# Two transformer blocks on one core: the input loaded a second time with features on rows, and down products that open their own banks

## Chip, cores and metric

One Trainium2 chip, one of its cores. The metric is the device time of one execution in microseconds (us), given as the median of several runs; the execution under the profiler is one run more and has a time of its own.

## What is computed

The input x is 256 tokens by 1024 features, float32. The first block has two layers. Each adds a mixer and then a gated feed-forward network to a residual stream, with an RMS norm ahead of both:

```python
hn = rmsnorm(x, norm_mix_w[0])
x = x + mlstm_mixer(hn, ...)                # layer 0: chunkwise mLSTM, 4 heads
x = x + swiglu(rmsnorm(x, norm_ffn_w[0]), ffn_w_in[0], ffn_w_out[0])
... # layer 1: window attention, then swiglu again

def swiglu(h, w_in, w_out):
    gu = h @ w_in                           # 1024 -> 2 * 2816
    return (silu(gu[..., :2816]) * gu[..., 2816:]) @ w_out
```

The second block joins 16 further tokens to the result, makes one wide projection of it, runs two kinds of attention and mixes them. The change touches nothing of the second block.

## The kernel before

**Exactness from two halves.** Every float32 operand of a large product is split into a rounded part (`_hi`, type float32r, written by ACT) and a rest (`_lo`, written by DVE as raw minus hi). `mm3` (lines 452 to 456) then makes each product of three matmuls: hi·hi, hi·lo, lo·hi. A weight chunk is 1024 x 512 (2 MB); it lies in `w_raw` as two halves of 1 MB, one buffer each, is split into `w_hi`/`w_lo` by ACT and DVE, and the half's buffer is free for the next transfer once DVE has written its rest (`w_lo_ok`).

**Features on partitions.** The products need activations with features on the partitions (`x_hi`, `x_lo`: 8 tiles of 128 x 256, one per 128 features, index k). The tokens lie on rows in `h`, so PE turns each tile with two transposes through PSUM (`to_stationary`, lines 512 to 526), ACT writes the hi part out of PSUM with the norm's weight as a scale (`split_st`, line 1251), and DVE writes the rest (`rest_st`, line 1747). `streamed` (528 to 543) turns two tiles ahead, and then, for each k, turns tile k+2 and does the products of tile k. The norm's root per token is not applied here: it is multiplied in later, from the sums of squares.

**The opening.** SP issues in this order (lines 351 to 361): the identity (64 KB), the parameters (40.5 KB), the two row blocks of x (512 KB each), the first half of weight chunk 0 in two pieces of 512 KB, its second half (1 MB), the side weights of the gates (512 KB). Then `main(1)` issues the two halves of chunk 1, the first once the first half of chunk 0 is split (`w_lo_ok` 1), the second once all of it is (`w_lo_ok` 2); it is followed by side unit 1 and `main(2)`. ACT (lines 1278 to 1299) waits for x and the parameters, and then for each k writes x_hi tile k, and the hi part of the weights of tile k (line 1289, 128 x 512). Behind k = 2 and k = 3 it also takes the squares of the two row blocks (line 1294). Then it splits the side unit and the two halves of chunk 1 (line 1275). DVE (lines 1812 to 1833) writes x_lo and w_lo of each k (lines 1747 and 1816); after k = 7 it raises `w_lo_ok` to 2. Then come the side unit's rest, the rest of chunk 1's first half, the roots, and the rest of chunk 1's second half (line 1808). PE does the queries' products (`halves_tile`, chunk 0: 12 matmuls of 256 columns for each k), the gates' (lines 586 to 589), and the keys' (chunk 1, lines 590 to 600), first k = 0 to 3 for both halves of the columns, then k = 4 to 7.

**The feed-forward network** (`ffn`, lines 710 to 811, called for both layers). Its down products are summed over 11 blocks of 256 features into four PSUM banks (4 to 7). The sums are opened by zero products: 16 matmuls of 128 columns from a tile of zeros, each bank's first with start set (lines 772 to 776); all products of `down` (740 to 750) then add. The zero products stand behind the last product of the mixer (`mixer_rest`, 686 to 691) and ahead of the wait for both accumulator banks (787 and 788), which the last mixer product's result leaves when DVE has added it to `h` (line 1996). Behind that wait the first up products start, with two transposes ahead of each k (`first`, 778 to 798). Then a loop of four turns does blocks 1 to 8, each `up` followed by the `down` of the block before it.

Of the kernel before, what the change touches and what calls it, by code (L numbers as in the profile page):

```python
# [20 lines left out]
F32 = mybir.dt.float32  # L21
# [5 lines left out]
P = 128  # L27
# [99 lines left out]

ST_TILES = {"x0": 8, "m_out": 8, "f0": 8, "x1": 8, "a_out": 8, "f1": 8, "u": 8, "cqkv": 3, "o_mla": 8, "o_fox": 8, "mixed": 8}

# [34 lines left out]

def two_blocks(nc, w_main, w_side, params, rows, c_l0, c_l1, c_b2, ident_d, x_d, meta_d, pos_d, out_d):
    ctx = ExitStack()
    with ctx:
# [3 lines left out]
        def sem(name):  # L171
            return ctx.enter_context(nc.semaphore(name))
# [24 lines left out]
        ffn_nat = sb("ffn_nat", [P, 2, R, 256])  # L197
        zero_r = g_hi[:, 512:512 + P]
        arena = sb("arena", [P, 17232])
# [12 lines left out]
        def pcol(name, k=0, n=1):  # L212
# [9 lines left out]

        XN = ar(4224, R, D)

        mqT, mkT, m_kn = ar(0, H0, S), ar(1024, H0, S), ar(2048, R, H0, DK)
# [55 lines left out]
        q_hi_ok, q_lo_ok, r0_ok, r0_ps, gates_ps, mk_ps, mk_ok = (  # L281
            sem(n) for n in ("q_hi_ok", "q_lo_ok", "r0_ok", "r0_ps", "gates_ps", "mk_ps", "mk_ok"))
        w_landed = [sem("w_landed0"), sem("w_landed1")]
        w_hi_ok, w_lo_ok = sem("w_hi_ok"), sem("w_lo_ok")
# [16 lines left out]
        silu_ok, g_tp, g_hi_ok, g_lo_ok = sem("silu_ok"), sem("g_tp"), sem("g_hi_ok"), sem("g_lo_ok")  # L301
        zero_ok = sem("zero_ok")
        out_landed = sem("out_landed")
# [32 lines left out]
        def _(sp):  # L336
# [13 lines left out]

            sp.dma_start(ident[:, :], ident_d).then_inc(in_landed, 16)
            sp.dma_start(par[:, :], params).then_inc(in_landed, 16)
            for r in range(R):
                sp.dma_start(h[:, r, :], x_d[r * P:(r + 1) * P, :]).then_inc(x_landed[r], 16)
            first = w_raw[:, 0, :, :].rearrange("p k n -> p (k n)")
            sp.dma_start(first[:, 0:2 * CH], w_main[0, 0][:, 0:2 * CH]).then_inc(w_first, 16)
            sp.dma_start(first[:, 2 * CH:], w_main[0, 0][:, 2 * CH:]).then_inc(w_landed[0], 16)
            main_half(0, 1)
            sp.dma_start(s_raw[:, 0, :], w_side[0]).then_inc(s_landed[0], 16)
# [36 lines left out]
        def _(pool):  # L396
            pool.memset(stat[:, :], 1.0)
            pool.memset(zero_r.bitcast(F32), 0.0).then_inc(zero_ok, 1)
            pool.memset(row_1[0:H0, :, :], 1.0)
# [51 lines left out]
        def _(pe):  # L451
# [125 lines left out]

            def m_queries(i):
                return lambda k: halves_tile(C_MQ, ("mq", i), 2 * i, k)

            pe.wait_ge(in_landed, 32)
            for r in range(R):
                pe.wait_ge(x_landed[r], 16)
            streamed("x0", residual_rows, {}, [m_queries(0), m_queries(1)])
            pe.wait_ge(s_lo_ok, U_GATES + 1)
# [4 lines left out]
            for k0 in (0, KT // 2):  # L590
                for i in range(2):
                    for k in range(k0, k0 + KT // 2):
                        ins = halves_tile(C_MK, None, 2 * i, k, to=bank[6 + i])
                    if k0:
                        ins.then_inc(mk_ps, 1)
                    elif i == 0:
                        pe.wait_ge(r0_ok, 1)
                        for r in range(R):
                            turned = pe.transpose(bank[4][:, r * P:(r + 1) * P], stat[:, 24 + r:25 + r].to_broadcast([P, P]), ident[:, :])
                        turned.then_inc(r0_ps, 1)  # L600
# [109 lines left out]
            def ffn(layer, mixer, next_st):  # L710
# [28 lines left out]

                def down(f, parts=(0, 1)):  # L740
                    pe.wait_ge(g_lo_ok, FB * layer + f + 1)
                    for ks in parts:
                        slot = (u0 + ks) % 2
                        pe.wait_ge(s_lo_ok, u0 + 2 * f + ks + 1)
                        for r in range(R):
                            for cc in range(2):
                                ins = mm3(bank[4 + 2 * r + cc][:, :], ffh[:, ks, r * P:(r + 1) * P],
                                          ffl[:, ks, r * P:(r + 1) * P], s_hi[:, slot, cc * CH:(cc + 1) * CH],
                                          s_lo[:, slot, cc * CH:(cc + 1) * CH], False, False)
                        ins.then_inc(s_used, 1)  # L750
# [19 lines left out]


                pe.wait_ge(zero_ok, 1)
                for i in range(4):
                    for q in range(4):
                        pe.matmul(bank[4 + i][:, q * P:(q + 1) * P], zero_r, zero_r,
                                  start=(q == 0), stop=False)

# [19 lines left out]
                for r in range(R):  # L797
                    for k in (KT - 2, KT - 1):
                        first(k, r)
                with pe.Fori(0, (FB - 1) // 2 - 1) as i:  # L800
                    up(2 * i + 1, 1, True)
                    down(2 * i)
                    up(2 * i + 2, 2, True)
                    down(2 * i + 1)
# [404 lines left out]
        def _(act):  # L1209
# [50 lines left out]
            def x_tile(t, a=M):  # L1260
                return lambda k: t[:, k, a:L]
# [15 lines left out]

            act.wait_ge(zero_ok, 1)
            act.activation(stat[:, 30:31], stat[:, 30:31], ACT.Square)
            for r in range(R):  # L1280
                act.wait_ge(x_landed[r], 16)
            act.wait_ge(in_landed, 32)
            for k in range(KT):
                split_st("x0", x_tile(x_hi), lambda k: pcol("norm_mix0", k), ks=(k,))
                if k == 0:
                    act.wait_ge(w_first, 16)
                elif k in (2, 4):
                    act.wait_ge(w_landed[k // 4], 16)
                act.activation(w_hi[:, 0, k, :], w_raw[:, k // 4, k % 4, :], ACT.Copy).then_inc(q_hi_ok, 1)
                if k % 4 == 3:  # L1290
                    act.drain().then_inc(w_hi_ok, 1)
                if k in (2, 3):
                    r = k - 2
                    ins = act.activation(XN[:, r, :], h[:, r, :], ACT.Square, accum_out=stat[:, r:r + 1])
                    if r:
                        ins.then_inc(ss_ok, 1)
# [420 lines left out]
        def _(dve):  # L1717
# [93 lines left out]

            dve.wait_ge(in_landed, 32)
            for k in range(KT):
                rest_st("x0", x_tile(x_hi), x_tile(x_lo), lambda k: pcol("norm_mix0", k), ks=(k,))
                dve.wait_ge(q_hi_ok, k + 1)
                dve.tensor_tensor(w_lo[:, 0, k, :], w_raw[:, k // 4, k % 4, :], w_hi[:, 0, k, :], ALU.subtract).then_inc(q_lo_ok, 1)  # L1816
                if k % 4 == 3:
                    dve.drain().then_inc(w_lo_ok, 1)
            rest_side(0)
            rest_half(1, 1, 0)  # L1820
# [844 lines left out]
```

## Time and profile before

| | us |
|---|---|
| median of 3 runs | 983.17 (982.9 to 983.58) |
| the profiled execution, its own time | 983.27 |
| its span, first to last instruction | 981.5 |
| outside the span | 1.77 |
| PE busy | 948.9 |
| DVE busy | 587.1 |
| ACT busy | 479.3 |
| POOL busy | 27.4 |

The span is what the trace covers; the profiled execution is 0.10 us above the median. A busy PE may still run at either of two clocks: the granted clock is listed as a share of 2.4 GHz for any stretch.

### The profile page before, as it was taken

What the parts mean: (1) busy time and instruction counts of PE and PEld (TensorE: products, weight loads), DVE (VectorE), ACT (ScalarE), POOL (GpSimd) and SP (SyncE); (2) the same over time, 40 slices, a digit from 0 to 9 for tenths busy, and PEclk for the clock granted to TensorE, in tenths of its full rate; (3) what the DMA queues carried; (4) which work ended last, traced back from release to release, by engine and by line L of the source; (5) the groups of instructions that cost most, each with busy time, mean ns of one, the idle gap of its engine ahead of it and who ended that gap; (6) DMA issues with size and microseconds to landing.
All of it is one profiled execution on the core that took longest, in us unless ns stands there. A gap on an engine that the chain in (4) does not pass through costs nothing.

```text
span 981.5 us, 13783 instructions
## 1 busy us (share of the span) xinstructions
PE 948.9 (97%) x5083; PEld 786.9 (80%) x5083; DVE 587.1 (60%) x1076; ACT 479.3 (49%) x772; POOL 27.4 (3%) x42
## 2 busy tenths in 40 slices
PE   6999999999999999999999999999989999999996
PEld 5887677888888898878888888789967877888775
DVE  4876757654454688556554535777555556565665
ACT  5565556353443548354534334675344454444442
POOL 0014200000000000000000000000000000000001
PEclk9999999999999999999999999999989999999998
DMA  6642245545445322246554454313223242434441
GB/s 210 250 172 86 93 184 214 221 164 203 181 162 223 130 86 87 91 165 231 197 194 191 162 223 171 130 62 131 110 86 129 86 150 109 167 116 145 159 164 43
DMA packets 25317, 149.22 MB, mean 152 GB/s; under 512 B 2992, under 2 KB 3120, under 8 KB 11056
## 3 DMA queue, kind: packets, MB, share of 16 engines
q1 hardware_dynamic: 24624, 146.39, 40.9%
q0 software_dynamic: 640, 2.11, 0.7%
q8 instruction: 34, 0.56, 0.2%
q14 instruction: 19, 0.16, 0.0%
HBM read 147.45 MB, written 1.05 MB: 151 GB/s over the span
## 4 chain that ended last, share of the span: by engine, by line
PE 83%; DVE 9%; ACT 3%; issue 2%; DVEq 2%; DMA 1%; SPq 0%; ACTq 0%
PE bank L454 24%; PE bank L455 23%; PE bank L456 23%; DVE w_lo L1808 2%; PE bank L525 2%; DMA w_raw<-w_main_dram 1%; PE bank L1014 1%; PE bank L736 1%; DVE arena L2193 1%; PE bank L1029 1%; PE bank L1067 1%; PE bank L1049 1%; PE bank L1050 1%; DVE w_lo L1787 1%; PE bank L851 1%
## 5 line engine op out<-in xcount | busy, mean ns | idle before, releaser
L454 PE MATMUL bank<-w_hi,x_hi 128*128 128x512 f32 (+2 forms) x648 | 262.7, 405 | 2.3 <-DVE x_lo L1747 0.9
L455 PE MATMUL bank<-w_lo,x_hi 128*128 128x512 f32 (+2 forms) x648 | 253.7, 392 | 0.0
L456 PE MATMUL bank<-w_hi,x_lo 128*128 128x512 f32 (+2 forms) x648 | 252.2, 389 | 0.0
L454 PEld LDWEIGHTS bank<-w_hi,x_hi 128*128 128x128 f32 x648 | 122.3, 189 | 33.7 <-issue 6.2
L456 PEld LDWEIGHTS bank<-w_hi,x_lo 128*128 128x128 f32 x648 | 121.8, 188 | 27.2
L1722 DVE TENSOR_TENSOR w_lo<-w_raw,w_hi 128x2048 fp32r<-128x2048 f32 x50 | 113.8, 2290 | 44.9 <-ACT w_hi L1214 44.6
L455 PEld LDWEIGHTS bank<-w_lo,x_hi 128*128 128x128 f32 x648 | 122.1, 188 | 22.3
L1214 ACT ACTIVATE w_hi<-w_raw 128x2048 fp32r<-128x2048 f32 x54 | 102.3, 1914 | 41.7 <-DMA w_raw<-w_main_dram 35.7
L1808 DVE TENSOR_TENSOR w_lo<-w_raw,w_hi 128x2048 fp32r<-128x2048 f32 x51 | 116.2, 2284 | 5.4 <-ACT w_hi L1275 5.3
L1275 ACT ACTIVATE w_hi<-w_raw 128x2048 fp32r<-128x2048 f32 x50 | 94.8, 1906 | 12.8 <-DMA w_raw<-w_main_dram 12.3
L2065 DVE SCALAR_TENSOR_TENSOR ffn_nat<-bank,stat,ffn_nat 128x256 f32<-128x256 f32 x44 | 21.3, 484 | 113.8 <-ACT ffn_nat L1415 113.7
L1415 ACT ACTIVATE ffn_nat<-bank,stat 128x256 f32<-128x256 f32 x44 | 20.9, 474 | 137.7 <-PE bank L456 137.7
L454 PE MATMUL bank<-x_hi,w_hi 128*128 128x256 f32 (+1 forms) x272 | 80.1, 294 | 2.3 <-DVE w_lo L1816 1.8
L456 PE MATMUL bank<-x_hi,w_lo 128*128 128x256 f32 (+1 forms) x272 | 77.2, 284 | 0.0
L455 PE MATMUL bank<-x_lo,w_hi 128*128 128x256 f32 (+1 forms) x272 | 77.1, 284 | 0.0
L1491 ACT ACTIVATE arena<-arena,small 128x144 f32<-128x144 f32 x64 | 29.5, 462 | 80.7 <-DVE small L2170 80.7
L454 PE MATMUL bank<-s_hi,g_hi 128*128 128x512 f32 x166 | 65.4, 394 | 0.5 <-ACT arena L1235 0.5
L456 PE MATMUL bank<-s_hi,g_lo 128*128 128x512 f32 x166 | 65.5, 394 | 0.0
L455 PE MATMUL bank<-s_lo,g_hi 128*128 128x512 f32 x166 | 65.3, 393 | 0.0
L454 PEld LDWEIGHTS bank<-x_hi,w_hi 128*128 128x128 f32 x272 | 51.8, 190 | 6.4 <-issue 2.9
L454 PE MATMUL bank<-w_hi,s_hi 128*128 128x512 f32 x128 | 53.7, 420 | 1.9 <-DVE s_lo L1745 1.5
L2448 DVE COPY arena<-bank 128x384 f32<-128x384 f32 x32 | 17.8, 556 | 62.7 <-PE bank L1040 62.7
(356 smaller groups left out, 1512.3 us busy)
## 6 DMA issues: line engine op xcount, KB each, us to landing
w_raw<-w_main_dram SPq DMA_DIRECT2D x111, 1024.0 KB, 4.8
s_raw<-w_side_dram SPq DMA_DIRECT2D x51, 512.0 KB, 4.2
h<-x_dram SPq DMA_DIRECT2D x2, 512.0 KB, 3.8
w_raw<-w_main_dram SPq DMA_DIRECT2D x2, 512.0 KB, 7.3
arena<-rows_dram POOLq DMA_DIRECT2D x2, 512.0 KB, 4.2
out_dram<-arena SPq DMA_DIRECT2D x1, 512.0 KB, 2.6
out_dram<-arena SPq DMA_DIRECT2D x2, 256.0 KB, 2.1
arena<-c_b_dram POOLq DMA_DIRECT2D x1, 264.0 KB, 2.9
```

The source lines that it names most:

```text
L454: pe.matmul(out, ah, bh, start=first, stop=False)
L455: pe.matmul(out, ah, bl, start=False, stop=False)
L456: return pe.matmul(out, al, bh, start=False, stop=last)
L525: ins = pe.transpose(b[:, M + r * P:M + (r + 1) * P], src(r, k), ident[:, :])
L1214: act.activation(w_hi[:, slot, 4 * g:4 * g + 4, :], w_raw[:, g, :, :], ACT.Copy).then_inc(w_hi_ok, 1)
L1275: act.activation(w_hi[:, slot, 4 * g:4 * g + 4, :], w_raw[:, g, :, :], ACT.Copy).then_inc(w_hi_ok, 1)
L1415: act.activation(ffn_nat[:, 0, r, :], acc[(n0 + r) % 2][:, 0:256], ACT.Silu, scale=stat[:, 24 + r:25 + r]).then_inc(silu_ok, 1)
L1491: ins = act.activation(tiles(r), tiles(r), ACT.Exp, bias=small[:, s0 + 2 + r:s0 + 3 + r], accum_out=small[:, s0 + 4 + r:s0 + 5 + r])
L1722: dve.tensor_tensor(w_lo[:, slot, 4 * g:4 * g + 4, :], w_raw[:, g, :, :], w_hi[:, slot, 4 * g:4 * g + 4, :], ALU.subtract).then_inc(w_lo_o ...
L1808: dve.tensor_tensor(w_lo[:, slot, 4 * g:4 * g + 4, :], w_raw[:, g, :, :], w_hi[:, slot, 4 * g:4 * g + 4, :], ALU.subtract).then_inc(w_lo_o ...
L2065: dve.scalar_tensor_tensor(out=ffn_nat[:, 1, r, :], in0=acc[b_][:, 256:512], scalar=root_col(r), in1=ffn_nat[:, 0, r, :], op0=ALU.mult, op ...
L2448: dve.tensor_copy(pt[:, 0:384], bank[5][:, 0:384]).then_inc(pt_ok, 1)
```

## The change

There are two edits.

**The opening.** The host also lays x out with features on rows (`x_t`: 128 x (8 x 256)), and the kernel loads it into `xt`, in the part of `arena` that the queries and keys take later. ACT and DVE make x_hi and x_lo straight from `xt`. The 16 transposes of "x0" go away. x itself is still loaded, behind the weights of chunk 0, and its squares are taken behind k = 5 and k = 6. The identity is loaded behind x. PE, ACT and DVE wait for what each step needs.

**The down products.** The 16 zero products of each layer go away, with the tile of zeros. The first `down` sets start on the first matmul of each bank. For this the first turn of PE's loop is written out ahead of it, and the loop has three turns.

```diff
-            sp.dma_start(ident[:, :], ident_d).then_inc(in_landed, 16)
-            sp.dma_start(par[:, :], params).then_inc(in_landed, 16)
+            sp.dma_start(xt[:, 0:2, :].rearrange("p k t -> p (k t)"), x_t[:, 0:2 * S]).then_inc(xt_landed[0], 16)
+            sp.dma_start(par[:, :], params).then_inc(par_landed, 16)
+            first = w_raw[:, 0, :, :].rearrange("p k n -> p (k n)")
+            sp.dma_start(first[:, 0:2 * CH], w_main[0, 0][:, 0:2 * CH]).then_inc(w_first, 16)
+            sp.dma_start(xt[:, 2:KT, :].rearrange("p k t -> p (k t)"), x_t[:, 2 * S:]).then_inc(xt_landed[1], 16)
+            sp.dma_start(first[:, 2 * CH:], w_main[0, 0][:, 2 * CH:]).then_inc(w_landed[0], 16)
+            main_half(0, 1)
             for r in range(R):
                 sp.dma_start(h[:, r, :], x_d[r * P:(r + 1) * P, :]).then_inc(x_landed[r], 16)
-            first = w_raw[:, 0, :, :].rearrange("p k n -> p (k n)")
-            sp.dma_start(first[:, 0:2 * CH], w_main[0, 0][:, 0:2 * CH]).then_inc(w_first, 16)
-            sp.dma_start(first[:, 2 * CH:], w_main[0, 0][:, 2 * CH:]).then_inc(w_landed[0], 16)
-            main_half(0, 1)
+            sp.dma_start(ident[:, :], ident_d).then_inc(in_landed, 16)
             sp.dma_start(s_raw[:, 0, :], w_side[0]).then_inc(s_landed[0], 16)
...
-            pool.memset(stat[:, :], 1.0)
-            pool.memset(zero_r.bitcast(F32), 0.0).then_inc(zero_ok, 1)
+            pool.memset(stat[:, :], 1.0).then_inc(one_ok, 1)
...
-            pe.wait_ge(in_landed, 32)
-            for r in range(R):
-                pe.wait_ge(x_landed[r], 16)
-            streamed("x0", residual_rows, {}, [m_queries(0), m_queries(1)])
+            for k in range(KT):
+                pe.wait_ge(xt_lo, k + 1)
+                for i in range(2):
+                    halves_tile(C_MQ, ("mq", i), 2 * i, k)
...
                         pe.wait_ge(r0_ok, 1)
+                        pe.wait_ge(in_landed, 16)
...
-                def down(f, parts=(0, 1)):
+                def down(f, parts=(0, 1), first=False):
...
-                                          s_lo[:, slot, cc * CH:(cc + 1) * CH], False, False)
+                                          s_lo[:, slot, cc * CH:(cc + 1) * CH], first and ks == 0, False)
...
-                pe.wait_ge(zero_ok, 1)
-                for i in range(4):
-                    for q in range(4):
-                        pe.matmul(bank[4 + i][:, q * P:(q + 1) * P], zero_r, zero_r,
-                                  start=(q == 0), stop=False)
-
...
-                with pe.Fori(0, (FB - 1) // 2 - 1) as i:
+                up(1, 1, True)
+                down(0, first=True)
+                up(2, 2, True)
+                down(1)
+                with pe.Fori(1, (FB - 1) // 2 - 1) as i:
...
-            for r in range(R):
-                act.wait_ge(x_landed[r], 16)
-            act.wait_ge(in_landed, 32)
+            act.wait_ge(par_landed, 16)
             for k in range(KT):
-                split_st("x0", x_tile(x_hi), lambda k: pcol("norm_mix0", k), ks=(k,))
+                if k in (0, 2):
+                    act.wait_ge(xt_landed[k // 2], 16)
+                act.activation(x_hi[:, k, M:L], xt[:, k, :], ACT.Copy, scale=pcol("norm_mix0", k)).then_inc(xt_hi, 1)
...
-                if k in (2, 3):
-                    r = k - 2
+                if k in (5, 6):
+                    r = k - 5
+                    act.wait_ge(x_landed[r], 16)
                     ins = act.activation(XN[:, r, :], h[:, r, :], ACT.Square, accum_out=stat[:, r:r + 1])
...
-            dve.wait_ge(in_landed, 32)
+            dve.wait_ge(par_landed, 16)
             for k in range(KT):
-                rest_st("x0", x_tile(x_hi), x_tile(x_lo), lambda k: pcol("norm_mix0", k), ks=(k,))
+                dve.wait_ge(xt_hi, k + 1)
+                dve.scalar_tensor_tensor(out=x_lo[:, k, M:L], in0=xt[:, k, :], scalar=pcol("norm_mix0", k), in1=x_hi[:, k, M:L],
+                                         op0=ALU.mult, op1=ALU.subtract).then_inc(xt_lo, 1)
...
+            dve.wait_ge(in_landed, 16)
             rest_side(0)
```

The semaphores' counts of turned tiles no longer include "x0".

## Rows read from the trace of the kernel before

**Rows 1.** Page, busy time by engine: busy us (share of the span) xinstructions.

```profile
PE 948.9 (97%) x5083; PEld 786.9 (80%) x5083; DVE 587.1 (60%) x1076; ACT 479.3 (49%) x772; POOL 27.4 (3%) x42
```

**Rows 2.** Chain that ended last, in order of time: start us, us, what.

```profile
2.60 6.91 DMA w_raw<-w_main_dram
...
10.94 0.58 PE bank L454
...
21.77 0.69 DVE w_lo L1816
22.54 6.88 DMA w_raw<-w_main_dram
...
31.39 2.29 DVE w_lo L1808
...
40.38 0.47 PE bank L454
```

**Rows 3.** DMA issues from 0 to 5 us: count, KB each, median us to landing.

```profile
h<-x_dram SPq DMA_DIRECT2D x2, 512.0 KB, 3.8
w_raw<-w_main_dram SPq DMA_DIRECT2D x2, 512.0 KB, 7.3
w_raw<-w_main_dram SPq DMA_DIRECT2D x1, 1024.0 KB, 9.7
```

**Rows 4.** Timeline of SP, 0 to 60 us: start us, us, what.

```profile
3.55 0.51 SPq L340 DMA_DIRECT2D w_raw<-w_main_dram  x1
```

**Rows 5.** Stretches of 1 us, core 0: busy by engine, granted clock, DMA share, GB/s.

```profile
7.00:8.00 1.00, 0.62 (x3) 0.21 (x1) 0.10 (x1) 0.47 (x1) 0.00 (x0) 1.00 0.91 217
...
12.00:13.00 1.00, 1.00 (x6) 1.00 (x6) 0.87 (x2) 0.96 (x2) 0.00 (x0) 1.00 0.97 397
```

**Rows 6.** Groups by line, 0 to 60 us: busy us, mean ns, idle before.

```profile
L1816 DVE TENSOR_TENSOR w_lo<-w_raw,w_hi 128x512 fp32r<-128x512 f32 x8 | 5.5, 690 | 2.0 <-ACT w_hi L1289 1.8
L1289 ACT ACTIVATE w_hi<-w_raw 128x512 fp32r<-128x512 f32 x8 | 5.0, 623 | 1.8 <-DMA w_raw<-w_main_dram 1.8
...
L1251 ACT ACTIVATE x_hi<-bank,par 128x256 fp32r<-128x256 f32 x8 | 3.7, 468 | 7.7 <-PE bank L525 7.6
...
L1294 ACT ACTIVATE arena<-h 128x1024 f32<-128x1024 f32 x2 | 2.1, 1056 | 0.1
...
L1294 ACT ACTIVATION_READ_ACCUMULATOR arena<-h 128x1 f32 x2 | 0.4, 191 | 0.0
```

**Rows 7.** Timeline, opening: PE's products of chunk 0, gates and keys.

```profile
11.75 0.41 PE L454 MATMUL bank<-x_hi,w_hi 128*128 128x256 f32 x1
...
12.39 0.41 PE L454 MATMUL bank<-x_hi,w_hi 128*128 128x256 f32 x1
...
14.37 0.29 PE L454 MATMUL bank<-x_hi,w_hi 128*128 128x256 f32 x1
...
14.73 0.28 PE L454 MATMUL bank<-x_hi,w_hi 128*128 128x256 f32 x1
...
24.81 0.28 PE L454 MATMUL bank<-x_hi,s_hi 128*128 128x256 f32 x1
...
33.73 0.39 PE L454 MATMUL bank<-x_hi,w_hi 128*128 128x256 f32 x1
```

**Rows 8.** Timeline, 134 to 137 us: the zero products of layer 0.

```profile
135.09 1.90 PE L775 MATMUL bank<-g_hi 128*128 128x128 f32 x16
...
135.29 0.69 DVE L1996 TENSOR_TENSOR h<-h,bank 128x512 f32<-128x512 f32 x1 [1.33 <-PE bank L456]
...
136.83 0.40 PE L525 MATMUL bank<-ident,h 128*128 128x128 f32 x2
```

**Rows 9.** Waits of PE, 134 to 380 us, longest: us, times, longest us.

```profile
PE bank L736 <- DVE w_lo L1787: 0.4, 1, 0.4
```

**Rows 10.** Stretches of 4 us on both sides of 116 us, columns as in rows 5.

```profile
112.00:116.00 4.00, 2.31 (x14) 1.53 (x12) 3.29 (x11) 1.56 (x5) 0.00 (x0) 1.00 0.22 92
116.00:120.00 4.00, 4.00 (x14) 3.14 (x13) 2.69 (x7) 2.31 (x5) 0.00 (x0) 0.57 0.02 4
```

More of the change, by code:

```diff
@@ L125 @@
 A_HALVES = {0: (C_AOUT, 0), 4: (C_AOUT, 1), 7: (C_AOUT + 1, 0)}
-ST_TILES = {"x0": 8, "m_out": 8, "f0": 8, "x1": 8, "a_out": 8, "f1": 8, "u": 8, "cqkv": 3, "o_mla": 8, "o_fox": 8, "mixed": 8}
+ST_TILES = {"m_out": 8, "f0": 8, "x1": 8, "a_out": 8, "f1": 8, "u": 8, "cqkv": 3, "o_mla": 8, "o_fox": 8, "mixed": 8}
 LAST = {("fk", 3): C_FK, ("fk", 7): C_FK + 1, ("fq", 3): C_FQ, ("fq", 7): C_FQ + 1}
@@ L162, with two_blocks @@
 RMS = {n: i for i, n in enumerate(("x0", "hs01", "hs23", "f0", "meta", "x1", "f1", "fin", "u", "cqkv", "post0", "post1"))}
-def two_blocks(nc, w_main, w_side, params, rows, c_l0, c_l1, c_b2, ident_d, x_d, meta_d, pos_d, out_d):
+def two_blocks(nc, w_main, w_side, params, rows, c_l0, c_l1, c_b2, ident_d, x_d, x_t, meta_d, pos_d, out_d):
     ctx = ExitStack()
@@ L197, in two_blocks @@
         ffn_nat = sb("ffn_nat", [P, 2, R, 256])
-        zero_r = g_hi[:, 512:512 + P]
         arena = sb("arena", [P, 17232])
@@ L223, in two_blocks @@
         XN = ar(4224, R, D)
+        xt = ar(0, KT, S)
         mqT, mkT, m_kn = ar(0, H0, S), ar(1024, H0, S), ar(2048, R, H0, DK)
@@ L282, in two_blocks @@
             sem(n) for n in ("q_hi_ok", "q_lo_ok", "r0_ok", "r0_ps", "gates_ps", "mk_ps", "mk_ok"))
+        par_landed, xt_landed = sem("par_landed"), [sem("xt_landed0"), sem("xt_landed1")]
+        xt_hi, xt_lo = sem("xt_hi"), sem("xt_lo")
         w_landed = [sem("w_landed0"), sem("w_landed1")]
@@ L301, in two_blocks @@
         silu_ok, g_tp, g_hi_ok, g_lo_ok = sem("silu_ok"), sem("g_tp"), sem("g_hi_ok"), sem("g_lo_ok")
-        zero_ok = sem("zero_ok")
+        one_ok = sem("one_ok")
         out_landed = sem("out_landed")
@@ L576, in halves_tile @@
                 return ins
-            def m_queries(i):
-                return lambda k: halves_tile(C_MQ, ("mq", i), 2 * i, k)
-            pe.wait_ge(in_landed, 32)
-            for r in range(R):
-                pe.wait_ge(x_landed[r], 16)
-            streamed("x0", residual_rows, {}, [m_queries(0), m_queries(1)])
+            for k in range(KT):
+                pe.wait_ge(xt_lo, k + 1)
+                for i in range(2):
+                    halves_tile(C_MQ, ("mq", i), 2 * i, k)
             pe.wait_ge(s_lo_ok, U_GATES + 1)
@@ L1275, in split_half @@
                 act.activation(w_hi[:, slot, 4 * g:4 * g + 4, :], w_raw[:, g, :, :], ACT.Copy).then_inc(w_hi_ok, 1)
-            act.wait_ge(zero_ok, 1)
+            act.wait_ge(one_ok, 1)
             act.activation(stat[:, 30:31], stat[:, 30:31], ACT.Square)
-            for r in range(R):
-                act.wait_ge(x_landed[r], 16)
-            act.wait_ge(in_landed, 32)
+            act.wait_ge(par_landed, 16)
             for k in range(KT):
-                split_st("x0", x_tile(x_hi), lambda k: pcol("norm_mix0", k), ks=(k,))
+                if k in (0, 2):
+                    act.wait_ge(xt_landed[k // 2], 16)
+                act.activation(x_hi[:, k, M:L], xt[:, k, :], ACT.Copy, scale=pcol("norm_mix0", k)).then_inc(xt_hi, 1)
                 if k == 0:
@@ L2655 @@
         "c_l0_dram": l0, "c_l1_dram": l1, "c_b2_dram": b2, "ident_dram": eye, "x_dram": i["x"][0],
+        "x_t_dram": i["x"][0].T.reshape(KT, P, S).transpose(1, 0, 2).reshape(P, KT * S),
         "meta_dram": i["meta_tokens_2"], "pos_dram": i["positions"].reshape(1, S),
```

## The prediction

> **What bounds the kernel now.** I read the page first. PE is busy for 948.9 us of the span of 981.5 [rows 1], so time is won where PE stands idle, does work that can go, or is held up by one chain; the change touches one place of the first kind and two of the second. Next the chain that ended last, in order of time, for the opening [rows 2]. Up to 10.94 us it is the way of the first weight piece, and PE makes its first product there. Around 21.8 it is not on PE: DVE writes the last rest of chunk 0 (21.77 + 0.69 = 22.46), which frees the buffer for the second half of chunk 1; that transfer takes 6.88 us, then ACT and DVE split it (DVE from 31.39 to 33.68), PE goes on with the keys at 33.73 [rows 7], and the DVE work behind it leads to PE at 40.38. **So the opening ends when DVE is through with chunk 0, and this is what I follow.** Then the issues of the first 5 us with their landing times, against SP's timeline [rows 3, 4]: the second half of chunk 0 is issued at 3.55, lands 9.7 later, at 13.25, and SP's transfers land in order. For the zero products I read the timeline around them [rows 8], and for what comes after them PE's waits through the first feed-forward network [rows 9].
>
> **The sum** is made against the profiled execution, 983.27 us, which is 0.10 above the median, 983.17. A measurement of this kernel can tell some 0.2%, 2.0 us, from no change.
>
> **Opening, transfers.** By SP's order, what stands up to and with the second half of chunk 0 is 3.25 MB before (identity 0.07, parameters 0.04, x 1.05, weights 2.10) and 3.19 MB after (x_t 1.05 in place of x, no identity). The issue is one place earlier. So that half lands at about 13.2 again; the copy costs nothing up to there. The first weight piece has 0.8 MB less ahead of it, some 2 us at 397 GB/s [rows 5], so it lands near 7.5 and not at 9.51 [rows 2]. The second piece keeps its place, about 11 (7.3 from an issue ahead of 3.55, rows 3 and 4). x follows: each block is 0.52 MB, 1.3 us at 397 GB/s, so 14.6 and 15.9. The identity and the gates' weights add 0.59 MB: 17.4.
>
> **Opening, ACT and DVE.** Before, each k waits for PE to turn a tile; x_hi had 7.7 us of such waits [rows 6]. After, ACT waits for transfers alone. The price of x_hi out of SBUF is not in the trace. A bound above is the one out of PSUM, 0.47; one below comes from line 1289 (512 columns, 0.62) and the squares (1024, 1.06): 0.85 ns a column, 0.41 for 256. I take 0.47, the row of the same shape. A k is then 0.47 + 0.62 = 1.09 on ACT. From the second half at 13.2: weights of k = 4 until 13.9; k = 5 until 15.0; squares of the first block (1.06 + 0.19 = 1.25) until 16.2, its x there at 14.6; k = 6 until 17.3; squares until 18.6, x there at 15.9; k = 7 until 19.7. DVE's rest takes 0.69 more: 20.4. Before it was 22.46. **The opening gains 2.1 us.**
>
> **Does it arrive?** The transfer of chunk 1's second half is issued 2.1 us earlier and is priced at its 6.88 again. The first half is issued when DVE is through with k = 3 (k = 2 starts when the second piece is there: 11.0 + 0.62 + 1.09 + 0.69, about 13.4), stands behind 17.4, needs 2.6 us for 1.05 MB, and lands near 20.0; ACT asks for it after the side unit, at 19.7 + 1.06 = 20.8. The cover is 0.8 us, and if it is gone, the rests behind it are late by what is over. SP waits for nothing new; x, identity and side unit stand behind the weights in its queue, each with the cover just worked out. POOL loses one memset.
>
> **Opening, PE.** A k is 12 matmuls of 256 columns. At first three start 0.64 us apart (11.75 to 12.39), later 0.36 (14.37 to 14.73) [rows 7]: these are the two clocks, 1.2 and 2.4 GHz, and a k costs 2.56 or 1.44. PE starts at 7.5 + 0.62 + 0.69, near 8.9. With one k at the lower clock as before it has ended k = 7 at 20.4 + 1.4 = 21.8, waiting for DVE towards the end, where before it began the gates at 24.81 [rows 7]. From there to the keys' second half is 8.9 us of PE work, so PE would be ready at 30.7, and the rest it needs is ready at 33.7 - 2.1 = 31.6. PE has 0.9 us in hand. Thus the 16 transposes in themselves give nothing more: what they give goes into this wait.
>
> Before, PE turned two tiles and more ahead of its first product (so `streamed` has it), and the products began at the lower clock all the same [rows 7]. The Trainium skill, "TensorE: Matmul & The Clock Gate", Part 4, says that transposes do not count as activity for the clock; the trace agrees, 0.64 us for three products at 11.75. By that rule nothing is lost with the transposes, which is the sum above; without it, one more k at the lower clock would cost 1.12, 0.2 of it past the 0.9 in hand.
>
> **Zero products.** The 16 stand from 135.09 and take 1.90 us on PE [rows 8]. Not all comes back. The mixer's last product has ended by 135.29, when DVE begins to add it to h; that lasts 0.69, and PE waits for it anyway before the first up product. DVE ends at 135.98, and with a handover of 0.08 (DVE ends at 22.46, SP issues at 22.54, rows 2) PE can go on at 136.06. Before, it did at 136.83. So 0.77 us a layer comes back, and 1.1 becomes a wait. What is late next: the x_hi tile of the transposes is needed only at k = 2, more than 2 us on. Behind them PE waits in the first network for 0.4 us at its longest [rows 9], on weights that are split in step with PE itself, so the gain lasts. Layer 1 has the same code with the same instructions. **Both layers: 1.5 us.** The bounds are 0, if something else ends that wait, and 2 x 1.90.
>
> **First turn written out.** It issues the same matmuls, with a flag set on four. I cost it at nothing, since PE streams through the old loop's turns with no wait that can be seen [rows 9]. Bounds: plus or minus 0.4 a layer, the longest wait there is.
>
> **The clock later on.** From 116 to 120 us the granted clock is 0.57 in the mean, most of it at the lower level, after PE was busy for 2.31 us of the 4 before [rows 10]. The clock not granted there is 0.43 x 4 = 1.7 us of work. The change moves it in time, and doesn't touch the idle ahead of it. I leave it at 0, with bounds of minus and plus 1.7.
>
> **The sum:** 983.27 - 2.1 - 1.5 = **979.7 us**.
>
> **Rivals.** *1. The opening is held by transfers.* The engines moved only 217 GB/s between 7 and 8 us [rows 5], with their share of time at 0.91. If x_t's 0.79 MB behind the first weight piece goes at that rate, it takes 3.6 us in place of 2.0, all that follows is 1.6 later, and the opening gains 0.5: 983.27 - 0.5 - 1.5 = 981.3. For it: a copy with rows of 2 and 6 KB is new in this queue. Against: the rate was back at 397 at 12 us. Chance 0.12.
>
> *2. The zero products were cover.* Their place is taken whole by another wait, such as one for the turned tiles: 983.27 - 2.1 = 981.2. Against: tiles 0 and 1 are turned under the mixer's last products, and no wait for them ends behind the zero products. Chance 0.08.
>
> *3. More than I sum.* The transfers land 0.7 us earlier, ACT works at 0.41 a tile, and the slow stretch behind 116 us falls away: 979.7 - 0.7 - 1.7 = 977.3. Chance 0.12.
>
> *4. Slower: PE's clock stays low.* Without turns to fill it, PE waits for DVE in each of the late steps of the opening. If the lower clock then holds for all eight, the queries take 8 x 2.56 = 20.5 us from 8.9 and end at 29.4, and not at 24.8: 4.6 later, with nothing of the opening's gain, so 983.27 + 4.6 - 1.5 = 986.4. It decides from the second slow k on (0.9 in hand against 1.12 each), and the gain of all is gone at about five. For it: the clock did fall behind idle time at 116 us [rows 10]. Against: PE has 1.44 us of products for each k, and ACT delivers one every 1.1 to 2.4 us. Chance 0.05. "TensorE: Matmul & The Clock Gate" of the Trainium skill, in its section on oscillation, describes just this, a product loop that waits for data in each step and falls back to the lower clock.
>
> *5. The edit does little:* as 1 and 2 together, 982.8, with chance 0.05.
>
> **How the numbers follow.** The forecast, 979.7, has 0.58. The range holds it and reaches to rival 3 below (977.3) and past 1 and 2 above (981.3 and 981.2, with some 0.1 for a handover more): 977.3 to 981.4. Rivals 4 and 5 and the tails are left out. Faster by over 0.2% is below 981.2: the forecast, rival 3 and half of 1 and 2, which lie on that line: 0.80. Within 0.2%: the other half and rival 5, 0.15. Slower: rival 4, 0.05.
>
> **What would show it.** PE's first product near 9 us and no transposes from h ahead of it. The second half of chunk 0 landing near 13.2, ACT's squares between k = 5 and k = 7, DVE's last rest of chunk 0 ending near 20.4, the next half of chunk 1 issued there, and PE at the keys' second half at 31.6. In each network, a wait of some 0.8 us on DVE's line 1996 in place of the zero products. The forecast is wrong if that last rest ends later than 22, if the transfer behind it takes much more than 6.88, or if the two networks' waits are as long as the zero products were.

## The result, and the profile of the changed kernel

The changed kernel takes 977.11 us in the median of 4 runs (976.44 to 977.72), the kernel before, timed beside it, 983.03 (982.27 to 983.58): the ratio is 0.994, with a 95% interval from 0.9923 to 0.9957. It is faster, as forecast, but by 5.9 us and not by 3.5; 977.11 lies 0.2 us below the end of the range. The profiled execution took 977.63 us. The page, span and busy time, to be held against [rows 1]:

```profile
span 975.8 us, 13669 instructions
...
PE 941.7 (97%) x5035; PEld 779.8 (80%) x5035; DVE 585.6 (60%) x1076; ACT 479.8 (49%) x772; POOL 27.3 (3%) x41
```

PE has 48 matmuls fewer: 16 transposes and 2 x 16 zero products. It is busy for 7.2 us less, the span is 5.7 us shorter.

The timeline of the changed kernel, opening: start us, us, engine, line, and in brackets the idle time before it and what ended it. Line numbers past the change differ: 1288 is 1289 of before, 457 is 454, 1818 is 1816, 600 is 599.

```profile
7.38 0.63 ACT L1288 ACTIVATE w_hi<-w_raw 128x512 fp32r<-128x512 f32 x1 [2.47 <-DMA w_raw<-w_main_dram]
...
8.88 0.55 PE L457 MATMUL bank<-x_hi,w_hi 128*128 128x256 f32 x1 [8.88 <-DVE w_lo L1818]
...
13.36 0.63 ACT L1288 ACTIVATE w_hi<-w_raw 128x512 fp32r<-128x512 f32 x1 [0.32 <-DMA w_raw<-w_main_dram]
...
13.89 0.49 ACT L1283 ACTIVATE x_hi<-arena,par 128x256 fp32r<-128x256 f32 x1
...
14.29 0.61 ACT L1288 ACTIVATE w_hi<-w_raw 128x512 fp32r<-128x512 f32 x1
...
14.35 0.36 PE L458 MATMUL bank<-x_lo,w_hi 128*128 128x256 f32 x1
...
18.87 0.69 DVE L1818 TENSOR_TENSOR w_lo<-w_raw,w_hi 128x512 fp32r<-128x512 f32 x1
...
19.63 0.33 SPq L342 DMA_DIRECT2D w_raw<-w_main_dram  x1
...
25.89 1.92 ACT L1274 ACTIVATE w_hi<-w_raw 128x2048 fp32r<-128x2048 f32 x1 [4.07 <-DMA w_raw<-w_main_dram]
...
28.43 0.38 PE L600 MATMUL bank<-ident,stat 128*128 128x128 f32 x2
...
28.84 0.42 DVE L1828 COPY arena<-bank 128x256 f32<-128x256 f32 x1 [1.91 <-PE bank L600]
...
29.34 2.29 DVE L1808 TENSOR_TENSOR w_lo<-w_raw,w_hi 128x2048 fp32r<-128x2048 f32 x1
...
31.69 0.38 PE L457 MATMUL bank<-x_hi,w_hi 128*128 128x256 f32 x1
...
38.35 0.47 PE L457 MATMUL bank<-w_hi,x_hi 128*128 128x512 f32 x1 [0.78 <-DVE w_lo L1722]
```

Three readings. The first product comes at 8.88 (10.94 in [rows 2]); the second half of chunk 0 is there at 13.36; the last rest of chunk 0 ends at 18.87 + 0.69 = 19.56 (22.46 before). From 13.36 to 14.29, one k takes ACT 0.93, though its rows last 0.63 and 0.49: a row begins before the one ahead of it has ended. And the last rest of chunk 1 (29.34, before 31.39) does not wait for the transfer. ACT is through with its half at 25.89 + 1.92 = 27.81; DVE stands at line 1828 for 1.91 us, waiting for PE to turn the norm's roots (line 600). Of the 2.9 us won at 19.56, 2.05 are left at 29.34, and 2.03 at 38.35 (40.38 in [rows 2]).

What PE waits for in the changed kernel (us in total, times, longest us); up to the gap of 0.78 at 38.35, the view lists only these two waits:

```profile
PE bank L457 <- DVE w_lo L1818: 8.9, 1, 8.9
...
PE bank L457 <- DVE w_lo L1722: 0.8, 1, 0.8
```

So from its first product, at 8.88, PE works through to the keys' second half, at 31.69, with pauses of some 0.2 us at most: 22.81 us. In the kernel before it does the same, from 10.94 to 33.73 [rows 2, 7]: 22.79 us. In both kernels it is PE that sets the length of the opening.

DVE's wait for the turned roots stood in the trace of the kernel before too, where the prediction did not look: its timeline has

```profile
29.44 1.92 ACT L1275 ACTIVATE w_hi<-w_raw 128x2048 fp32r<-128x2048 f32 x1 [4.71 <-DMA w_raw<-w_main_dram]
...
30.89 0.42 DVE L1825 COPY arena<-bank 128x256 f32<-128x256 f32 x1 [1.05 <-PE bank L599]
```

There ACT ended the half at 31.36, and DVE the copy at 31.31: transfer and PE came out together, and the prediction took the transfer for all of it.

The zero products' place in the changed kernel, timeline, to be held against [rows 8]:

```profile
132.14 0.69 DVE L1999 TENSOR_TENSOR h<-h,bank 128x512 f32<-128x512 f32 x1 [0.63 <-PE bank L459]
...
132.93 0.41 PE L528 MATMUL bank<-ident,h 128*128 128x128 f32 x2 [0.83 <-issue]
```

PE goes on 0.10 us after DVE ends. The profile puts the wait down to "issue", so it names no releaser; DVE's line 1999 ends just ahead of it. Of the 1.90 us a layer, 0.83 became this wait.

The granted clock behind 116 us, stretches of 4 us in the changed kernel, columns as in [rows 5], to be held against [rows 10]:

```profile
112.00:116.00 4.00, 2.71 (x15) 2.19 (x16) 3.68 (x9) 2.78 (x7) 0.00 (x0) 1.00 0.00 0
116.00:120.00 4.00, 4.00 (x18) 3.00 (x16) 3.89 (x5) 0.98 (x2) 0.00 (x0) 1.00 0.27 70
```

PE has the same gaps here as before (0.65 and 1.03 us, now from 111.6 to 113.9), but the clock does not fall behind them. Setting equal instructions of the two profiled executions against each other, the changed kernel is 1.9 us ahead at 114, 3.2 at 130, 3.9 behind the first zero products, 4.6 behind the second, and 5.3 behind 733, where the stretch at the lower clock is longer in the kernel before. So in this pair the opening and the zero products give 3.3 of the 5.7, about as forecast, and the clock gives most of the rest. Whether the change did that was the question for the experiments.

### The profile page after: what moved, and what is told of

It is laid out like the page before. It is cut to its first block, busy times and chain, and to the rows that moved or that the text cites. A ratio compares the mean times of both kernels' runs of the same rounds, so it can differ in the third digit from the quotient of the medians.

```text
span 975.8 us, 13669 instructions
## 1 busy us (share of the span) xinstructions
PE 941.7 (97%) x5035; PEld 779.8 (80%) x5035; DVE 585.6 (60%) x1076; ACT 479.8 (49%) x772; POOL 27.3 (3%) x41
## 3 DMA queue, kind: packets, MB, share of 16 engines
HBM read 148.50 MB, written 1.05 MB: 153 GB/s over the span
## 4 chain that ended last, share of the span: by engine, by line
PE 83%; DVE 9%; ACT 3%; issue 2%; DVEq 2%; DMA 1%; SPq 0%; ACTq 0%
PE bank L457 24%; PE bank L458 23%; PE bank L459 23%; DVE w_lo L1808 2%; PE bank L528 1%; PE bank L1013 1%; PE bank L737 1%; DVE arena L2196 1%; PE bank L1028 1%; PE bank L1066 1%; PE bank L1049 1%; PE bank L1048 1%; DVE w_lo L1787 1%; PE bank L850 1%; DMA w_raw<-w_main_dram 1%
## 5 line engine op out<-in xcount | busy, mean ns | idle before, releaser
L457 PEld LDWEIGHTS bank<-x_hi,w_hi 128*128 128x128 f32 x272 | 52.4, 193 | 13.2 <-issue 11.7
```

Of the source, the lines that this page charges most:

```text
L457: pe.matmul(out, ah, bh, start=first, stop=False)
```

## The experiments

### Each part alone

The new opening with the old zero products and loop:

```diff
+                for i in range(4):
+                    for q in range(4):
+                        pe.matmul(bank[4 + i][:, q * P:(q + 1) * P], zero_r, zero_r,
+                                  start=(q == 0), stop=False)
...
-                up(1, 1, True)
-                down(0, first=True)
-                up(2, 2, True)
-                down(1)
-                with pe.Fori(1, (FB - 1) // 2 - 1) as i:
+                with pe.Fori(0, (FB - 1) // 2 - 1) as i:
```

> The opening as changed, the zero products and the loop as before. Theory A (the opening gives 2.0 us, as the trace of the changed kernel shows at PE's first product of the values, and the low clock behind 116 us goes away because the idle ahead of it comes 2 us earlier): 983.0 - 2.0 - 1.3 = 979.7 us, granted clock 1.00 from 112 to 120 us. Rival B (the low clock behind 116 us has nothing to do with the opening; it comes and goes from run to run, or went with the zero products): 981.0 us, with the low clock in some runs.

Measured: 979.44 us beside 982.89, ratio 0.9964 (0.995 to 0.9978). That is 3.5 us, by the interval 2.2 to 4.9; 2.1 was forecast. In its profile the clock stays at 1.00 from 112 to 120 us, as theory A had it.

The kernel before with the other edit, no zero products and the turn written out (the same lines the other way round).

> The opening as before, the zero products gone and the first turn of the loop written out. Both theories price the two networks at 0.75 us each. Theory A: nothing ahead of 116 us moves, so the low clock there stays; 981.5 us, and up to 0.5 less if the low stretch near 720 us gets shorter. Rival B (the zero products' removal brings the missing 2 us): 979.5 us or below.

Measured: 980.99, ratio 0.9984 (0.9975 to 0.9993): 1.6 us, by the interval 0.7 to 2.5, where 1.5 was forecast. Its profile has the clock at 1.00 behind 116 too, so theory A missed there. In its timeline PE's wait is the forecast one again:

```profile
133.95 0.39 PE L454 MATMUL bank<-w_hi,s_lo 128*128 128x512 f32 x1
135.17 0.41 PE L523 MATMUL bank<-ident,h 128*128 128x128 f32 x2 [0.83 <-issue]
```

The parts add up to 5.1 by their ratios, 5.4 by their medians, beside 5.9 for both together. The term that was too small is the opening.

### Is the later clock a matter of phase?

18 of the 24 products of the gates are done twice, some 2.1 us of PE work ahead of line 600, in each kernel; bank 5 is opened anew afterwards.

```diff
+            for k in range(6):
+                mm3(bank[5][:, 0:S], s_hi[:, 0, k * P:(k + 1) * P], s_lo[:, 0, k * P:(k + 1) * P],
+                    x_hi[:, k, M:L], x_lo[:, k, M:L], k == 0, k == 5)
```

> The changed kernel with 18 of the 24 gate products done twice, so that PE is busy without a gap and all that follows comes about 2.1 us later, near to where it was before the change. Theory A (when the idle comes decides on the clock): the low stretch behind 116 us is back, 977.1 + 2.1 + 1.3 = 980.5 us. Rival B: only the added work counts, 979.2 us, clock as in the changed kernel.

> The kernel before with the same 18 products done twice: all that follows comes about 2.1 us later. Theory A: the low stretch behind 116 us changes with the time at which the idle comes; if it goes away, 983.0 + 2.1 - 1.7 = 983.4 us, if it only moves, 985.1 us. Rival B: 985.1 us with the low stretch 2.1 us later.

Measured: the changed kernel 978.41, ratio 0.9961 (0.9947 to 0.9976); the kernel before 986.3, ratio 1.0035 (1.0023 to 1.0048). The stretch behind 116 is in neither profile. One profile of each can't settle the question, since the stretch turned out to come in some executions only (below). What the pair shows is PE's chain: DVE's wait for the turned roots grew to 3.2 us in both, and the last rest of chunk 1 came late with it (30.20 and 34.37). In the changed kernel the keys' second half comes 24.11 us behind the first product; in the profile with nearly the same length of the lower clock (the second repeat below) it is 22.06, so the added work goes through to PE's end of the opening. In time it cost some 1.4 us here and 3.4 in the kernel before; this difference is not explained.

### PE's clock in the opening

Products ahead of the first real ones, into a bank that is opened later: of zeros, 72 in the kernel before and 96 in the changed one; or of x_hi's tile 0 with itself, 8 in the kernel before and 16 in the changed one.

```diff
+            for _ in range(96):
+                pe.matmul(bank[7][:, 0:P], zero_r, zero_r, start=True, stop=True)
...
+            pe.wait_ge(xt_hi, 1)
+            for _ in range(16):
+                pe.matmul(bank[7][:, 0:S], x_hi[:, 0, M:M + P], x_hi[:, 0, M:L], start=True, stop=True)
```

"Swap" puts DVE's last rest of chunk 1 ahead of its wait for the turned roots:

```diff
             dve.drain().then_inc(r0_ok, 1)
+            rest_half(1, 1, 1)
             dve.wait_ge(r0_ps, 1)
...
-            rest_half(1, 1, 1)
```

> The kernel before, with 72 products of zeros on PE ahead of the first transposes, so that the clock is up when the products begin. Theory A (before the change PE paces ACT and DVE through the turned tiles, so each us at the low clock in the opening makes it 0.5 us longer, and runs have 3 to 6 us of it): 982.8 - 2.2 = 980.6 us. Rival B (the opening's end is set by DVE and transfers, low clock or not): 982.8 us.

> The changed kernel with 96 products of zeros on PE ahead of the first product. Theory A (after the change ACT and DVE run free of PE; PE's low clock costs only what goes past its cover): 977.1 - 0.6 = 976.5 us, so that the change is worth 4.1 us with the clock up from the start in both. Rival B (low clock costs both kernels the same): as much less as in the kernel before.

> As the last, and DVE makes the rest of chunk 1's second half ahead of its wait for the turned roots, not behind it. Theory A: the rest begins when ACT is through with the half, near 27.8 us, in place of 28.4 to 29.3; PE reaches the keys' second half some 0.5 us earlier, 976.0 us. Rival B (the transfer alone sets the end): no difference to the last.

These three missed: 990.1, 989.91 and 987.4 us. The zeros did not bring the clock up, and so lasted far past the first data. The timeline of PE in the changed kernel with zeros:

```profile
1.05 20.74 PE L585 MATMUL bank<-g_hi 128*128 128x128 f32 x96 [1.05 <-POOL g_hi L403]
21.59 0.52 PE L459 MATMUL bank<-x_hi,w_hi 128*128 128x256 f32 x1
...
25.26 0.28 PE L461 MATMUL bank<-x_hi,w_lo 128*128 128x256 f32 x1
```

20.74 / 96 = 0.216 us each to the end, where the 16 of [rows 8] took 0.119; the products behind them still ran at the lower clock and rose only near 25.2. The miss shows what sets the end. In the changed kernel with zeros DVE was through with chunk 0 at 19.21 and ACT with the next half at 25.97, no later than without them (19.25 and 27.37 in the changed kernel timed beside it); PE's first product came at 21.59, 13.0 us later than there (8.56), and the time is 13.0 us longer (989.91 beside 976.88). The swap gained 2.5 us here (to 987.4): without it, DVE waits 14.07 us for the turned roots ahead of that rest.

> The kernel before, with 8 more products of the first tile of x_hi with itself on PE while it waits for the first weights; they go nowhere. Theory A (PE paces ACT and DVE through the turned tiles, and real products ahead bring the rise of the clock forward by their 1.7 us): 982.5 - 0.85 = 981.6 us. Rival B (DVE and transfers set the opening's end, low clock or not): 982.5 us.

> The changed kernel, with 16 more products of the first tile of x_hi with itself on PE while it waits for the first weights, from about 4.9 us on. Theory A (the clock rises 3 to 4 us earlier; what PE then gains in the opening is up to 1.8 us, of which only what goes past its cover counts, 0 to 0.9): 976.5 us. Rival B: the full 1.8 us, 975.2 us.

The real products did it. PE's timeline of the changed kernel with 16 of them:

```profile
5.33 3.51 PE L583 MATMUL bank<-x_hi 128*128 128x256 f32 x16 [5.33 <-ACT x_hi L1286]
8.67 0.28 PE L457 MATMUL bank<-x_hi,w_hi 128*128 128x256 f32 x1
8.79 0.28 PE L458 MATMUL bank<-x_lo,w_hi 128*128 128x256 f32 x1
```

0.12 from start to start is the higher clock from the first product on. The last rest of chunk 1 starts at 27.41 (29.34 in the changed kernel), and the kernel takes 975.81 us beside 982.86, ratio 0.9932 (0.992 to 0.9945). It is the fastest of all, by some 1.2 us on the changed kernel, whose interval it overlaps. In the kernel before, 8 such products took the rest from 31.39 to 30.55, but nothing was left at the end: 982.17, ratio 1.0002 (0.9992 to 1.0012). The waits of PE between 10 and 60 us show where it went:

```profile
PE bank L454 <- DVE w_lo L1725: 1.9, 2, 1.1
```

PE waited for rests of chunk 2, and those for a transfer that landed at 39.4, where it had landed at 38.6 in the kernel before, though issued 0.8 earlier. One profile shows this; why the transfer was slower is open.

> The changed kernel, in which DVE makes the rest of chunk 1's second half ahead of its wait for the turned roots. Theory A (DVE stands idle from 26.9 to 28.8 us while ACT is through with that half at 27.8): the rest ends 1 us earlier and the roots' row takes its place behind it, 976.5 us. Rival B (PE is the bound there): 977.0 us.

> The two last together. Theory A: both gains, 975.8 us. Rival B: no more than the better of the two.

Measured: 976.9 (ratio 0.994, 0.9927 to 0.9953) and 975.99 (0.9936, 0.9924 to 0.9948). The rest starts earlier, at 27.22 and 26.86, but the time is what it is without the swap. So the rest, freed of its wait, ends ahead of PE, and PE remains what sets the end, as rival B had it. At 65 us the swapped kernel is 0.7 ahead of the mean of the changed one; its median does not show it.

### The same kernels again

The changed kernel, timed once more, and then both kernels profiled again, side by side on another chip, all unchanged.

> The changed kernel once more, unchanged, for the sizes of the others of this call and for the length of the low clock in its opening. Theory A and rival B: 977.1 us, with the first product near 8.9 us and the rise of the clock 3 to 6 us behind it.

Measured: 976.88 beside 982.16, ratio 0.9942 (0.9929 to 0.9954).

> The kernel before, unchanged. Theory A, the stretch at the lower clock behind 116 us belongs to the kernel before (the change took it away): it stands here again, 116 to 120 us, granted clock near 0.57 in the mean, and about 1.2 to 1.7 us are lost in it. Theory B, it comes in some executions and not in others: of three repeats at least one has 116 to 120 at 1.00 and a shorter time by about 1.2 us. For the opening: theory C, the first profile's opening was a typical one: the third rest of chunk 1 starts at 31.4 within 0.2; theory D, it was a good one: 31.7 to 32.3.

> The kernel before, unchanged, a second repeat; A and C: lower clock behind 116 us, rest of chunk 1's second half starting at 31.4; B and D: the stretch there in one repeat and not in another, the rest starting between 31.4 and 32.3.

> The kernel before, unchanged, a third repeat; A and C: lower clock behind 116 us, rest of chunk 1's second half starting at 31.4; B and D: the stretch there in one repeat and not in another, the rest starting between 31.4 and 32.3.

> The changed kernel, unchanged, for a third profile. A: granted clock 1.00 behind its 3.5 us gap at 111.6 to 114.1. B: in some profile of it a stretch of about 1.7 us lost there. C and D say alike: rest of chunk 1's second half starting between 28.4 and 29.4.

Measured: the kernel before takes 981.65, 982.08 and 980.97 us, the changed one 977.36. In none of the three repeats of the kernel before does the clock fall behind 116. The first repeat's stretches of 4 us:

```profile
112.00:116.00 4.00, 2.31 (x12) 1.46 (x11) 3.21 (x12) 1.57 (x4) 0.00 (x0) 1.00 0.27 113
116.00:120.00 4.00, 3.98 (x20) 3.30 (x21) 3.88 (x8) 2.57 (x6) 0.00 (x0) 1.00 0.01 4
...
720.00:724.00 4.00, 2.77 (x7) 1.37 (x8) 1.08 (x1) 0.23 (x1) 0.00 (x0) 0.66 0.39 121
724.00:728.00 4.00, 4.00 (x21) 3.32 (x20) 1.09 (x3) 2.99 (x3) 0.00 (x0) 0.91 0.35 145
```

and the second place in the execution that the prediction was summed from:

```profile
720.00:724.00 4.00, 1.86 (x5) 0.97 (x6) 1.99 (x1) 1.08 (x5) 0.00 (x0) 0.56 0.22 45
724.00:728.00 4.00, 4.00 (x16) 2.97 (x15) 0.68 (x1) 2.02 (x3) 0.00 (x0) 0.59 0.54 221
```

PE is busy for the same 2.31 us ahead of 116 as in [rows 10], and here the clock stays at 1.00. So that stretch comes in some executions and not in others: in 2 of the 8 profiles with the old opening, in none of the 10 with the new one. The executions that were only timed say more, as the mean granted clock of each is on record. The two profiles with the stretch read 0.992 in the mean, all others 0.994 to 0.997. Of 43 timed executions of the kernel before (two far outliers left out), 13 read 0.992; they took 983.11 to 984.01 us, 983.55 in the mean. The other 30 read 0.994 or more and took 981.0 to 983.57, 982.16 in the mean. Of the 47 executions with the new opening, with or without other edits, none reads 0.992. The mean does not tell where the clock was low, but the counts go against chance alone: the stretch was rarer, or gone, with the new opening. Why isn't shown, and the 11 executions with the old opening and without the zero products have no 0.992 either. In the mean of the 43 it is worth 0.4 us. The one near 720 comes in all, at one of two lengths: 1.7 us of clock not granted, or 3.4. The changed kernel had 1.7, 3.4 and 3.4 there in its three profiles; the kernel before 3.4 in the first and 1.7 in each repeat.

Start times (us) of the same six ACT instructions in each profile:

| | third table load | s_hi, mixer | fourth table load | x_hi, layer 1 | next w_hi | last part |
|---|---|---|---|---|---|---|
| before, as summed | 64.68 | 114.59 | 143.11 | 424.70 | 689.87 | 961.04 |
| before, repeat 1 | 64.91 | 114.82 | 142.06 | 423.69 | 688.89 | 959.29 |
| before, repeat 2 | 65.44 | 115.31 | 142.53 | 424.11 | 689.31 | 959.73 |
| before, repeat 3 | 64.57 | 114.43 | 141.65 | 423.25 | 688.45 | 958.74 |
| after | 62.80 | 112.73 | 139.24 | 420.10 | 684.98 | 955.39 |
| after, repeat 1 | 62.58 | 112.47 | 138.98 | 419.90 | 684.68 | 956.35 |
| after, repeat 2 | 61.35 | 111.27 | 137.79 | 418.69 | 683.46 | 955.12 |
| means, repeats of before less after | 2.7 | 2.7 | 3.4 | 4.1 | 4.5 | 3.6 |

Read by the last row, the opening gives 2.7 and each layer's zero products 0.7. Ahead of the stretch near 720 the change has gained 4.5; that 3.6 are left at the end is the longer stretch there in two of the changed kernel's three profiles. The first row stands out: it starts like the repeats, and is 1.0 behind their mean from the fourth table load on and 1.8 behind it at the end.

For the opening the repeats lie between the two theories on record: the last rest of chunk 1 starts at 31.61, 32.14 and 31.25 in the kernel before, mean 31.67, so the first profile, 31.39, was on the good side by 0.3. In the changed kernel it starts at 29.34, 28.69 and 27.97. This follows the length of the lower clock at its start: PE's first products last 5.5, 4.6 and 3.8 us at it. The last of the three, 27.97, is below what was expected (28.4 to 29.4).

The opening as PE goes through it, in us; the last column goes up to the first product whose row is shorter than 0.40:

| | first product | keys' second half | between | of it at the lower clock |
|---|---|---|---|---|
| before, as summed | 10.94 | 33.73 | 22.79 | 3.0 |
| before, repeat 1 | 10.41 | 33.96 | 23.55 | 4.2 |
| before, repeat 2 | 10.64 | 34.49 | 23.85 | 5.3 |
| before, repeat 3 | 10.61 | 33.60 | 22.99 | 3.4 |
| after | 8.88 | 31.69 | 22.81 | 5.5 |
| after, repeat 1 | 8.56 | 31.03 | 22.47 | 4.6 |
| after, repeat 2 | 8.26 | 30.32 | 22.06 | 3.8 |

By means, repeats of before less after: the first product comes 2.0 us earlier and the keys' second half 3.0. The 1.0 between is PE's own work: ten transposes stood between the products.

## Why the prediction was wrong

The direction and the zero products were right. The path of the opening was wrong, and with it the opening's term came out too small; and the sum was made against an execution that was long by chance.

**"PE has 0.9 us in hand."** This step failed: PE had nothing in hand, before or after. The prediction followed transfers, ACT and DVE, and gave PE a wait at the keys' second half. But its own rows have none: 24.81 + 8.9 = 33.7 is when PE went on in the kernel before. DVE's rest ends just then because DVE, ahead of it, copies roots that PE turns in the middle of its products; the step left out that copy. So "the 16 transposes in themselves give nothing more: what they give goes into this wait" fails too. There is no such wait, and their absence shortens PE's work by about 1.0 us, on top of the 2.0 by which the first product is earlier. Together that is 3.0 where 2.1 stood; 2.7 are left at 65 us, and alone the opening measured 3.5 by the medians (2.2 to 4.9). The runs bear the path out: work added on PE, or PE's late start, goes through to the end, and taking away DVE's wait changes nothing that the median shows.

**31.6 was luck.** The forecast for the end of that rest agrees with 29.34 + 2.29 = 31.63 in the first profile. The lower clock lasted 2.5 us longer there than in the profile that was summed ("one k at the lower clock as before" became about two, 8.88 to 14.35 at 2.56 each). That costs some 1.2 us (half of it, an estimate) and hides what the transposes give. In the repeats PE rose earlier, the rest ended at 30.98 and 30.26, and so the opening gave more than in the first profile.

**"A k is then 0.47 + 0.62 = 1.09 on ACT."** It is 0.93, as the rows of ACT overlap, and the squares took 1.05 from start to start where 1.25 stood. The trace of the kernel before had it: two rows of line 1289 with an x_hi between them start at 10.42 and 11.30. With it chunk 0 ended at 19.56 (repeats 19.25 and 18.94), and not at 20.4. The landing times held: ACT began with the weights at 7.38 where 7.5 stood, and the second half was there at 13.36 where 13.2 stood. The transfer behind it took 6.26 us up to ACT's start, not 6.88. By these, DVE could have begun its last rest at 27.8. It waited for PE, so none of this set the end.

**"I leave it at 0."** The lower clock behind 116 and near 720 was taken for a fixed part of the kernel. It differs from execution to execution: the sum was made against 983.27, and three repeats took 981.57 in the mean, for the same work. 981.57 - 3.6 = 978.0 would have met the changed kernel's profiled executions, 977.63, 978.57 and 977.36, but also by luck: the gain had reached 4.5, and 0.9 of it went into the longer stretch near 720. The bound of minus 1.7 belonged mostly to the base of the sum. To a smaller part it may belong to the change, as the stretch behind 116 was not seen with the new opening; 0.4 us in the mean is not 1.7, since most executions of the kernel before do without the stretch.

What stays open: over all timed executions the means differ by 5.5 (982.58 - 977.12, ten of the changed kernel), and by 5.0 without those that read 0.992; the profiled ones by 3.7 at the end (981.57 - 977.85) and by 4.5 ahead of 720. The profiles are three of each kernel, and single times of the kernel before spread from 981.28 to 984.01 on one chip, so a remainder of this size may be chance. The runs do not show it.

**Zero products**, 1.5 forecast, 1.6 alone: right, with 0.83 us of wait where 0.8 stood. **The first turn written out**, at nothing: nothing shows behind it; the longest of PE's waits for split weights in the networks went from 0.4 to 0.5.

**The rivals.** The opening was not held by transfers (1), nor were the zero products cover (2). The number came out near rival 3's, 977.3, with two of its three reasons to be seen: the stretch at 116 was missing, and a tile took ACT 0.40 from start to start, though its row lasted 0.49. But ACT did not set the end, and the transfers were not earlier. Of rival 4, PE did stay at the lower clock for two k, but not because it waited for DVE in each step: it didn't wait. "TensorE: Matmul & The Clock Gate" of the Trainium skill, Part 4, says that transposes do not count as activity for the clock. The trace agrees: with three pairs of transposes ahead, the repeats of the kernel before ran low for 3.4 to 5.3 us from their first product, without them the changed kernel for 3.8 to 5.5.

## What to carry to other kernels

Before giving an engine time in hand, look for its pauses: one that works through a stretch without any, as PE did here, sets its end, whichever chain is followed. Where two chains meet at one instruction, follow both back: a short wait (here 1.05 us, DVE for turned roots) names the second chain. Before summing against one profile, take it again, and read the mean granted clock of every timed execution: two executions of the same kernel differed by 2.3 us here, as much as the larger edit was to bring. For an engine that starts each instruction before the last one's row has ended, add up starts and not durations.

## What the runs showed of the chip that was not expected

Products of zeros for 20.74 us left PE at its lower clock (0.216 us each to the last), while 16 products of real data with 256 columns, 3.51 us, were followed by products at the higher clock at once. They differ in data and in columns, and the runs do not tell which of the two counts. The length of the lower clock at the start is no constant either: from 2.9 to 5.9 us from the first real product, over the profiles of kernels with no products added ahead of it. Behind the same idle time in the middle of a kernel, with 2.31 us of busy PE in the 4 us ahead of it, the clock fell in one execution and stayed up in another.
